# Placing the split weights at another offset from the streamed activations, modulo 256 bytes

## The reference, cut to what matters

```python
h = rmsnorm(x, norm_pre_w)                       # (256, 2048)
proj = h @ w_in                                  # 2048 x 16400: q k v o z_a (i f) u z_b g_a g_b
...                                              # conv + silu on q, k; mLSTM per head; pooling
merged = sigmoid(g_a) * (y_a @ w_proj_mlstm) + sigmoid(g_b) * (y_b @ w_proj_pool)
x = x + rmsnorm(merged @ w_out, norm_post_w)
hn = rmsnorm(concat(meta, x), attn_norm_w)       # (272, 2048) and padding
proj = hn @ w_in_2                               # q k v gates, latent q and kv
...                                              # two kinds of attention, 8 heads each
h = h + concat(oA, oB) @ w_out_2
y = rmsnorm(h, final_norm_w)
```

## Time and profile before

| | |
|---|---|
| median of 3 runs | 1513.9 us (1513.66 to 1516.12) |
| the profiled execution | 1519.33 us, with a span of 1517.5 us |
| mean granted clock of TensorE | 0.993 of full |
| TensorE busy with matmuls (PE) | 97% of the span |
| VectorE, ScalarE, GpSimd busy | 55%, 47%, 4% |
| share of 16 DMA engines taken by the main queue | 54.3% |

### The profile page before, as it was taken

The page is one execution under the profiler, slowest core; times in us unless marked ns, Lnnn a source line. Parts: engine busy times, 40 slices in busy tenths (PEclk is TensorE's granted clock), DMA queues, the critical chain, the costliest instruction groups (busy, mean ns, idle before and its releaser), DMA issues.

```text
span 1517.5 us, 27814 instructions
## 1 busy us (share of the span) xinstructions
PE 1473.8 (97%) x10848; PEld 1390.9 (92%) x10848; DVE 839.2 (55%) x1032; ACT 711.2 (47%) x931; POOL 66.2 (4%) x90
## 2 busy tenths in 40 slices
PE   6999999999999999999999999979999999999997
PEld 6999988899999999999999997868999988888886
DVE  5667655446655656554454544556444445556754
ACT  5554535445554434343343434455434344666542
POOL 0000000001010000000000001000000001111000
PEclk9999999999999999999999999989999999999999
DMA  7566555655556555666666657646555552333673
GB/s 274 169 194 191 171 178 167 207 164 155 159 164 189 171 176 168 192 184 187 185 185 184 186 181 251 193 143 216 183 164 161 175 166 86 111 98 111 200 216 125
DMA packets 70646, 264.80 MB, mean 174 GB/s; under 512 B 7840, under 2 KB 7840, under 8 KB 69408
## 3 DMA queue, kind: packets, MB, share of 16 engines
q1 hardware_dynamic: 69552, 254.24, 54.3%
q0 software_dynamic: 1024, 9.57, 1.7%
HBM read 259.58 MB, written 4.19 MB: 174 GB/s over the span
## 4 chain that ended last, share of the span: by engine, by line
PE 93%; DVE 2%; ACT 2%; DMA 2%; issue 1%; DVEq 0%; POOL 0%; ACTq 0%; SPq 0%; POOLq 0%
PE ps L323 23%; PE ps L327 23%; PE ps L325 23%; PE ps L313 6%; PE ps L314 5%; PE ps L315 5%; PE ps L422 2%; DMA metan<-in_meta 1%; PE ps L661 1%; PE ps L495 1%; PE ps L503 1%; PE ps L668 1%; DVE wl L1104 1%; PE ps L666 0%; DMA xn<-in_x 0%
## 5 line engine op out<-in xcount | busy, mean ns | idle before, releaser
L1104 DVE TENSOR_TENSOR wl<-raw,wh 128x1024 fp32r<-128x1024 f32 x474 | 579.9, 1227 | 557.8 <-ACT wh L810 550.1
L810 ACT ACTIVATE wh<-raw 128x1024 fp32r<-128x1024 f32 x474 | 499.4, 1060 | 548.5 <-PE ps L327 425.0
L323 PE MATMUL ps<-xh,wh 128*128 128x256 f32 x1792 | 503.9, 281 | 1.6 <-DVE xl L1119 1.6
L325 PE MATMUL ps<-xl,wh 128*128 128x256 f32 x1792 | 500.3, 279 | 0.0
L327 PE MATMUL ps<-xh,wl 128*128 128x256 f32 x1792 | 499.9, 279 | 0.0
L323 PEld LDWEIGHTS ps<-xh,wh 128*128 128x128 f32 x1792 | 336.5, 188 | 2.3 <-DVE xl L1119 2.0
L325 PEld LDWEIGHTS ps<-xl,wh 128*128 128x128 f32 x1792 | 336.0, 187 | 0.3
L327 PEld LDWEIGHTS ps<-xh,wl 128*128 128x128 f32 x1792 | 336.1, 188 | 0.0
L323 PE MATMUL ps<-x2h,wh 128*128 128x256 f32 (+1 forms) x688 | 198.4, 288 | 3.5 <-ACTq L923 3.3
L327 PE MATMUL ps<-x2h,wl 128*128 128x256 f32 (+1 forms) x688 | 194.8, 283 | 0.0
L325 PE MATMUL ps<-x2l,wh 128*128 128x256 f32 (+1 forms) x688 | 194.4, 283 | 0.0
(11 more groups left out here) (321 smaller groups left out, 1776.4 us busy)
## 6 DMA issues: line engine op xcount, KB each, us to landing
raw<-in_w_stream SPq DMA_DIRECT2D x474, 512.0 KB, 3.7
xn<-in_x SPq DMA_DIRECT2D x2, 1024.0 KB, 6.2
xr<-in_x POOLq DMA_DIRECT2D x1, 2048.0 KB, 16.4
x_kept<-xr POOLq DMA_DIRECT2D x1, 2048.0 KB, 9.2
x1r<-x_kept POOLq DMA_DIRECT2D x1, 2048.0 KB, 10.1
out<-yn SPq DMA_DIRECT2D x4, 512.0 KB, 2.7
poolw<-in_pool_w POOLq DMA_DIRECT2D x1, 1024.0 KB, 5.7
postw<-in_post_w POOLq DMA_DIRECT2D x1, 1024.0 KB, 8.1
```

The costliest lines, as they stand in the source:

```text
L323: pe.matmul(out_at(j), whr[:, c, f], hi[:, kc, tokens], start=st, stop=False, skip_group_check=True)
L325: pe.matmul(out_at(j), whr[:, c, f], lo[:, kc, tokens], start=False, stop=False, skip_group_check=True)
L810: act.activation(slot_view(wh_at[r], layout), raw[r][:, :, :], ACT.Copy).then_inc(wh_done, 1)
L1104: tt(slot_view(wl_at[r], layout), raw[r][:, :, :], slot_view(wh_at[r], layout).bitcast(F32), ALU.subtract).then_inc(split_done, 1)
```

## The change

Two layouts take the place of `BY_FEATURE`, all activations and constants move up by 64 bytes, and the layouts by token and of the second block move with them.

- `BY_FEATURE` is now (52, 512): residue 80. The activations are at residue 192, so the moving chunk is at the weights' address plus 112.
- `SHIFTED` is (56, 512): residue 96, and the moving chunk is at the weights' address plus 96. It holds for the first slot of each group by feature, and in OZ for slot 3 too. That makes 51 slots, with the first of V and of WO; 235 have (52, 512).
- `BY_TOKEN` is (16, 512): residue 192 on both sides, offset 0 as before. The first three slots of V and WO now take the first three layouts of the stage ahead.
- `SECOND` goes from (0, 528) to (16, 528) and moves with the activations: its offsets stay. `SECOND_KEYS` goes from (16, 528) to (0, 528): its offsets of 192 and 64 change places, slot by slot.

No engine gets another instruction, and none is moved: TensorE's list has 6286 rows on either side, and the operations and sizes in them are the same. Only addresses differ.

```diff
-BY_FEATURE, BY_TOKEN, SECOND, SECOND_KEYS = (48, 512), (0, 512), (0, 528), (16, 528)
+BY_FEATURE, SHIFTED = (52, 512), (56, 512)
+BY_TOKEN, SECOND, SECOND_KEYS = (16, 512), (16, 528), (0, 528)
...
 def slot_layouts():
 
-    out = []
+    out, last = [], []
     for name, kinds, times in STAGES:
-        of = [LAYOUT_OF.get(kind, BY_FEATURE) for kind in kinds for _ in range(slots_of(kind))] * times
+        of = [LAYOUT_OF.get(kind, SHIFTED if k == 0 or name == "OZ" and k == 3 else BY_FEATURE)
+              for kind in kinds for k in range(slots_of(kind))] * times
         if name in ("V", "WO"):
-            of[:LEAD] = out[-LEAD:]
+            of[:LEAD] = last[:LEAD]
         out += of
+        last = of
     return out
...
-    R_X, R_C, R_Y, R_Z, R_V, R_T = 51200, 86016, 118784, 151552, 167936, 184384
+    R_X, R_C, R_Y, R_Z, R_V, R_T = 51264, 86080, 118848, 151616, 168000, 184448
...
         first, pitch = layout
-        return slot[:, first:first + SLOT_KC * pitch].rearrange("p (c n) -> p c n", n=pitch)[:, :, 0:COLS]
+        return slot[:, first:first + SLOT_KC * COLS].rearrange("p (c n) -> p c n", n=COLS) if pitch == COLS else bass.AP(
+            slot[:, 0:1].tensor, first, [[SLOT_W, P], [pitch, SLOT_KC], [1, COLS]])
```

## The result

The changed kernel takes 1529.18 us (median of 6 runs, 1525.03 to 1533.39); the kernel before, run beside it, 1514.38 us. The ratio is 1.0086, with a 95% interval of 1.0064 to 1.0108: slower by 14.8 us as a difference of the medians (13 us by the ratio), where 28 us less were forecast. Rival C, the bad offset, had 1528 us as its lower end, and that is what came.

A forecast was written before the change was run, and what follows sets the result against it. TensorE's matmul stream was taken to bound the kernel (in flight 97% of the span). A gain of 28 us from the new offsets, all other parts 0, gave 1513.9 - 28 = 1486 us; 8-in-10 range 1455 to 1519.

The forecast's parts named there:

- Rival C: Every first-block slot by feature: new offset is bad and slower, 14 to 42 us, at the lower end 1528; chance 0.17.
- The pace is a matter of addresses: V, AK, OZ: pace is at least partly a matter of addresses; in V 6.6 ns a matmul for offset alone.
- Two steps at one offset, settled where the stream starts: OZ at offset 64: the same instructions have two paces, 113.3 and 117.8 ns, settled where the stream starts.
- Part 1: First-block slots by feature: 6290 matmuls at 117.8 ns go to 113.3 at the new offsets, 28 us gained.
- It also fits the part of the change that sets the first slot apart: First slots of groups: a separate start offset would matter where OZ shows the two paces part; no size given.
- Part 2: First three slots of V and WO, offset 192 to 160 or 144: 0.5 us either way, taken as 0.
- Part 3: By token elsewhere and second block: offsets stay, or change places and cancel; 0.
- Part 4: Split's writes at multiples of 16 bytes: even 10% longer, 0.1 us more a slot of each, hidden.
- Part 5: Weight stream gets faster with TensorE, 193 GB/s; transfers land in time, so hidden.
- B: Change does not do it: slow step as often as before, or pace independent of offset; 1514 us; chance 0.13.
- D: Fast step found in some groups, lost in others; gain some 14 us, 1500; counted with the forecast, together 0.44.
- A: Stream at offsets 96 and 112 faster than any so far: at 108.8 ns 58 us gained, 1456; chance 0.26.

The follow-up runs named there:

- all64: Changed kernel with every slot by feature at offset 64 again, the first ones too; ratio 1.0004 against the kernel before.
- all192: Changed kernel with every slot by feature at offset 192; ratio 0.999 against the kernel before.
- alternate64_192: Changed kernel with slots by feature at offset 64 in even slots and 192 in odd ones; 1493.62 us, ratio 0.9838 against the kernel before.
- both32_off64: Changed kernel with all slots by feature at offset 64, activations and weights both 32 bytes on from the kernel before; ratio 0.9995 against that kernel.

## Why the prediction was wrong, by its own steps

- **What bounds the kernel**: right. All of the difference is in the pace of the stream, in the stages named.
- **The pace is a matter of addresses**: right, and now shown by undoing it (all64) and by sixteen offsets. The rule quoted from the Trainium skill ("SBUF — State Buffer", "SBUF: two separate sides"), that TensorE never waits on anyone, speaks of one engine against another and not of two reads of the same engine. Taken as the prediction took it, as a pace that knows no addresses, it would give a ratio of 1; 1.0091 for offset 112 and 0.9838 for 64 and 192 by turns disagree. The gap that the Trainium skill gives for an isolated matmul in "TensorE: Matmul & The Clock Gate", "Back-to-back issue gap", 109.2 ns at 256 columns, was reached at no offset in this stream; the best was 113.3.
- **Two steps at one offset, settled where the stream starts**: right, with the addition that a change of layout under a running stream can settle it anew, and the better part of the result. all192 has both in one kernel at one layout, and the forms with passages make use of it.
- **Part 1, the pace at offset 112**: this is the step that failed. I took 113.3 ns, "the nearest row (same operands, same shape, only another step of the two readers)". That row was of offset 64; nearness of shape stood in for the one quantity that the change altered. Measured: 120.0 ns, 2.2 above the old pace, where 4.5 below was forecast. 2.2 x 6290 = 14 us; the 326 matmuls that had been fast in OZ lost 6.7 ns each, 2 us more. The measured 14.8 is a little less, since the first two slots of most groups ran at 119.6 to 119.9 and parts of QK and UZ at 118.3. The upper bound of this part came from V, and its rows do not carry over either. In V the layouts at 192 and at 144 both cost 233.3 ns, that at 64 cost 228.9 (all192) and offset 0 is the best, 226.7; by feature offset 0 is among the worst, 120.0.
- **"It also fits the part of the change that sets the first slot apart"**: wrong. It took the shape of the edit for evidence that 96 leads into a fast step. With 96 ahead of 112 or of 64, MG stays in the slow step of either. The idea as such does work, from 64 to 192.
- **Part 2, V and WO**: nothing, as taken: V 89.6 us in both, WO 109.2 and 108.9.
- **Part 3, the second block**: right; G, AK and AV as long as before. AK's two slot times changed places.
- **Part 4**: right. Writes at 16 bytes past a line cost nothing: ScalarE's median is 1060 ns and VectorE's 1225 against the earlier trace rows.

```profile
L1108 DVE TENSOR_TENSOR wl<-raw,wh x474: 1201/1225/1639, 13.2 to 1513.6; 128x1024 fp32r<-128x1024 f32 x158
...
L814 ACT ACTIVATE wh<-raw x474: 1037/1060/1108, 10.9 to 1512.5; 128x1024 fp32r<-128x1024 f32 x158
```

- **Part 5**, a faster weight stream, was not put to the test by the changed kernel, whose TensorE became slower. In alternate64_192 it was, and it held: 193 GB/s, and TensorE had a matmul in flight throughout MG (304.74 of 304.74 us).
- **Rivals B and D** needed 117.8 or 113.3 ns at offset 112; neither pace appeared there. **A** needed less than 113.3, which no offset gave.
- **Rival C** had the outcome and, by luck, the price. AK's 2.3 ns lie between the offsets 64 and 192 at 272 columns, both of which have the same two paces at 256; that 112 costs 2.2 ns more than 64 does not follow from them. Its mechanism, a start off the boundary of the weight reader's lines, is not shown and in part contradicted: both32_off64 had the weights off a 64-byte line at no cost, and offset 0, on such a boundary, is as slow as 112. Its chance, 0.17, was too small: of the sixteen offsets none but 64 and 192 showed 113.3, and nothing in the trace before said that 112 was like either.

What stays open: why offset 112 has a slower pace than 64, beyond the fact that it has. That the two sides are the streaming chunk and the next weight load is argued from the addresses, not shown. No run took the weight load away. Nor is it shown why the passage from 64 to 192 turns the step, or why the paces are what they are.

## What to carry to other kernels

Where a dense stream of fp32r matmuls has a pace above columns over clock, look at the offset between the moving chunk and the stationary operand modulo 256 bytes (the table above holds for 256 columns by feature; V, with 512, orders its offsets otherwise): read the pace slot by slot, not from a matmul's own duration, and measure offsets before believing in one. Look for two paces at the same addresses; if the faster one exists, a layout that changes by turns can bring the stream back to it after each interruption. An offset that no row shows has no forecast; the nearest row in shape is not the nearest in the thing that is changed.

## What the runs showed of the hardware that was not expected

- A pace, once taken, holds exactly as long as the layout stays and no other matmuls break in: in all192 the last 62 slots of QK (1488 matmuls) at 113.3 ns, the 2688 matmuls of MG at 117.8. 113.33 ns are 272 periods of the 2.4 GHz clock, 120.0 ns are 288, and 117.78 ns are 848 for three matmuls. If a column takes one period, 16, 32 and on average 26.7 periods are lost for 256 columns.
- It need not hold where both addresses step by 64 modulo 256 and the offset stays. The second block's two chunks of a slot lie so, and the trace of the kernel before has the row in AQ, 256 columns wide. In a slot at offset 192 that follows one at 64, the first chunk's matmuls run at 113.3 ns (9 in 1.02 us) and the second chunk's at 117.8 again (9 in 1.06 us):

```profile
1186.69 0.28 PE L323 MATMUL ps<-x2h,wh 128*128 128x256 f32 x1
1187.71 0.28 PE L323 MATMUL ps<-x2h,wh 128*128 128x256 f32 x1
...
1188.06 0.28 PE L323 MATMUL ps<-x2h,wh 128*128 128x256 f32 x1
1189.12 0.28 PE L323 MATMUL ps<-x2h,wh 128*128 128x256 f32 x1
```

  The prediction read AK, but not these rows, which already show the passage from 64 to 192 at the shape in question. That moving both sides costs nothing is thus shown for a whole kernel moved, not for a step in the middle of a stream.
- Which paces there are depends on the difference of two addresses at a grain of at most 16 bytes: 48 gave 116.7 ns where 64 gave 117.8 or 113.3, and 80 gave 118.1.
- The stretches that are fast in OZ lie in the same slots in the kernel before, in all64 and in both32_off64. Such a step is not chance from run to run, but follows from what stands ahead of it.
